# A state-space scan beside the products: places for ScalarE's part, for z's units and for small steps of the second block

## The reference

```python
xn = rmsnorm_2(x, norm1_w[l])
p = xn @ w_in[l]
z, xbc, dt_raw, p_rwkv, p_hgrn, p_gate = jnp.split(p, in_splits, axis=-1)
...
def ssd_chunked(x, dt, a, bm, cm):          # c = 4 chunks of Q = 128 tokens, both directions
    a_cum = jnp.cumsum(dt * a.reshape(G, hg), axis=2)
    xdt = x * dt[..., None]
    seg = a_cum[:, :, :, None] - a_cum[:, :, None]
    lmat = jnp.exp(jnp.where(mask, seg, -jnp.inf))
    cb = jnp.einsum('bcqgn,bcsgn->bcqsg', cm, bm)
    y_diag = jnp.einsum('bcqsgh,bcsghp->bcqghp', cb[..., None] * lmat, xdt)
    chunk_states = jnp.einsum('bcsgn,bcsghp->bcghpn', bm, xdt * decay_to_end[..., None])
    ...
y = y_f + y_b + xs * d_skip[:, None]
y = y.reshape(b, L, SSM_INNER) * jax.nn.silu(z)
...
p = p + mu[0] * (prev - p) + mu[1] * (nxt - p)      # token shift of p_rwkv
```

## Time and profile before

| | |
|---|---|
| median of 3 runs | 3432.21 us (3430.88 to 3433.6) |
| profiled execution | 3431.43 us, its span 3429.9 us |
| TensorE busy | 3310.9 us, 97% of the span |
| VectorE busy | 2018.7 us, 59% |
| ScalarE busy | 1354.2 us, 39% |
| granted clock of TensorE, mean | 0.992 |

### The profile page before, as it was taken

One profiled execution on the slowest core, in us unless ns is written; L12 is line 12 of the kernel. 1 busy time (PEld: TensorE's weight loads), 2 busy tenths in 40 slices (PEclk: granted clock), 3 DMA queues, 4 the chain that ended last, 5 costly groups with the idle time before them and its releaser, 6 DMA issues.

```text
span 3429.9 us, 53077 instructions
## 1 busy us (share of the span) xinstructions
PE 3310.9 (97%) x21864; PEld 2720.9 (79%) x21864; DVE 2018.7 (59%) x3803; ACT 1354.2 (39%) x2604; POOL 0.2 (0%) x4
## 2 busy tenths in 40 slices
PE   7989999999999999999999999999999999999998
PEld 7777788888888777788888888777777788888887
DVE  6776753554436776753554438775766678664434
ACT  5456543342225466543343224434443324232222
POOL 0000000000000000000000000000000000000000
PEclk9999999999999999999999999999999999999999
DMA  4221223233324221223233334333411235433332
GB/s 141 80 70 50 56 74 105 92 99 98 98 99 127 86 64 50 57 79 105 86 105 99 96 101 118 89 92 106 125 38 40 92 95 157 135 97 94 97 98 86
DMA packets 353875, 315.31 MB, mean 92 GB/s; under 512 B 10288, under 2 KB 281776, under 8 KB 353636
## 3 DMA queue, kind: packets, MB, share of 16 engines
q1 hardware_dynamic: 352916, 309.75, 29.9%
q10 hardware_dynamic: 720, 2.16, 0.2%
HBM read 288.28 MB, written 23.59 MB: 91 GB/s over the span
## 4 chain that ended last, share of the span: by engine, by line
PE 80%; DVE 11%; ACT 5%; issue 3%; DMA 2%; SPq 0%; DVEq 0%; ACTq 0%
PE banks L532 14%; PE banks L534 13%; PE banks L533 13%; PE banks L427 8%; PE banks L429 8%; PE banks L428 8%; DVE weights_r L368 2%; PE banks L632 1%; ACT weights_high_r L361 1%; PE banks L2928 1%; PE banks L2867 1%; PE banks L1241 1%; PE banks L1228 1%; PE banks L1332 1%; PE banks L2881 1%
## 5 line engine op out<-in xcount | busy, mean ns | idle before, releaser
L368 DVE TENSOR_TENSOR weights_r<-weights,weights_high_r 128x1024 fp32r<-128x1024 f32 (+2 forms) x517 | 592.9, 1154 | 355.7 <-ACT weights_high_r L361 354.6
L532 PE MATMUL banks<-h_T_hi,weights_high_r 128*128 128x512 f32 (+2 forms) x1912 | 759.6, 397 | 10.6 <-DVE h_T_lo L881 4.7
L534 PE MATMUL banks<-h_T_hi,weights_r 128*128 128x512 f32 (+2 forms) x1912 | 737.9, 386 | 0.0
L533 PE MATMUL banks<-h_T_lo,weights_high_r 128*128 128x512 f32 (+2 forms) x1912 | 737.5, 386 | 0.0
L361 ACT ACTIVATE weights_high_r<-weights 128x1024 fp32r<-128x1024 f32 (+2 forms) x517 | 511.2, 1000 | 360.8 <-DMA weights<-in_w_mlp 213.3
L532 PEld LDWEIGHTS banks<-h_T_hi,weights_high_r 128*128 128x128 f32 x1912 | 361.4, 189 | 98.6 <-issue 28.8
L534 PEld LDWEIGHTS banks<-h_T_hi,weights_r 128*128 128x128 f32 x1912 | 361.2, 189 | 72.7
L533 PEld LDWEIGHTS banks<-h_T_lo,weights_high_r 128*128 128x128 f32 x1912 | 361.7, 189 | 68.0 <-issue 2.6
L427 PE MATMUL banks<-weights_high_r,h_T_hi 128*128 128x512 f32 (+2 forms) x672 | 279.3, 416 | 9.2 <-DVE gate L2208 3.7
L429 PE MATMUL banks<-weights_high_r,h_T_lo 128*128 128x512 f32 (+2 forms) x672 | 254.9, 379 | 0.0
L428 PE MATMUL banks<-weights_r,h_T_hi 128*128 128x512 f32 (+2 forms) x672 | 254.7, 379 | 0.0
(11 more groups left out here) (562 smaller groups left out, 5228.5 us busy)
## 6 DMA issues: line engine op xcount, KB each, us to landing
weights<-in_w_in SPq DMA_DIRECT2D x183, 512.0 KB, 3.8
weights<-in_w_mlp SPq DMA_DIRECT2D x128, 512.0 KB, 3.8
weights<-in_ffn_w_in SPq DMA_DIRECT2D x44, 512.0 KB, 3.8
weights<-in_w_out SPq DMA_DIRECT2D x24, 512.0 KB, 3.6
weights<-in_ffn_w_down SPq DMA_DIRECT2D x22, 512.0 KB, 3.5
weights<-in_w_mem_kv SPq DMA_DIRECT2D x16, 512.0 KB, 3.5
weights<-in_w_diff_o SPq DMA_DIRECT2D x16, 512.0 KB, 3.6
weights<-in_w_mla_o SPq DMA_DIRECT2D x8, 512.0 KB, 3.4
```

What stands on the lines that cost most here:

```text
L368: ve.e.tensor_tensor(self.part(c.w_raw_r, u), self.part(c.w_raw, u), self.part(c.w_high_r, u).bitcast(F32), ALU.subtract).then_inc(*ve.tel ...
L532: pe.e.matmul(out, lhsT=wh[:, k, :], rhs=hi[k][:, cols], start=(k == 0), stop=False)
L533: pe.e.matmul(out, lhsT=wh[:, k, :], rhs=lo[k][:, cols], start=False, stop=False)
L534: mm = pe.e.matmul(out, lhsT=wl[:, k, :], rhs=hi[k][:, cols], start=False, stop=(k == self.chunks - 1))
```

## The change

It changes where steps stand in the order, and no arithmetic:

- `Tokens` gets `in_a_row`: for z, two units of weights are used for one tile before the next tile's turn (u0t0, u1t0, u0t1, u1t1 in place of u0t0, u0t1, u1t0, u1t1).
- ScalarE's part of the scan becomes a stage of its own, `StateDecays`, whose steps are at the time of TensorE's step plus 0.6. They stood at the time of VectorE's step, which is 3 or 2 steps ahead of TensorE's.
- The scan's times are written out: the first 0.53 steps earlier, and 4.02 apart in place of 4.07.
- The memsets of the shift's pads become a stage (`ShiftPads`) that stands 0.45 steps behind the convolution's end and ahead of the scan's L2552.
- The second step of `Constants2` stands at 7.2 in place of 3.1, and the last turn of the norm at 5.2 in place of 7.

```diff
-            for u in self.units:
+            for some_units in (self.units[j:j + self.in_a_row] for j in range(0, len(self.units), self.in_a_row)):
                 for t in some:
-                    yield n, u, t, t == some[0], u == self.units[-1]
+                    for u in some_units:
+                        yield n, u, t, t == some[0], u == self.units[-1]
...
-    def act(self):
+    def decays_act(self):
         ac = self.c.ac
         ac.wait_ge("dta_low")
...
+class StateDecays(Stage):
+    def __init__(self, ssm):
+        self.n, self.act = ssm.n, ssm.decays_act
...
+class ShiftPads(Stage):
+    n = 1
...
+    def dve(self):
+        self.shift.pads_dve()
+        yield
...
+    def pads_dve(self):
+        ve = self.c.ve
+        ve.wait_all(self.free)
+        for n, y in enumerate(self.pad):
+            ve.e.memset(y[:, 0:1], 0.0).then_inc(*ve.step())
+            ve.e.memset(y[:, S + 1:S + 2], 0.0).then_inc(*ve.tell("shift_padded", n))
...
-        plan.at(k, (0.6, 3.1, 18.2))
+        plan.at(k, (0.6, 7.2, 18.2))
...
+        plan.at(ShiftPads(shift), (plan.now + 0.45,))
...
-            return Tokens(c, name, c.hT, KD, w[:, col:col + 512], sink, ready=normed, ring=ring, together=2)
+            return Tokens(c, name, c.hT, KD, w[:, col:col + 512], sink, ready=normed, ring=ring, together=2, in_a_row=2 if how == "silu" else 1)
...
-        plan.beside(ssm, scan_at, plan.now - 1.5, [3] * 6 + [2] * (ssm.n - 6))
+        scan_times = [scan_at - 0.03 + 4.02 * n for n in range(ssm.n)]
+        scan_lags = [3] * 6 + [2] * (ssm.n - 6)
+        plan.at(ssm, scan_times, scan_lags)
+        plan.at(StateDecays(ssm), (t + lag + 0.6 for t, lag in zip(scan_times, scan_lags)))
...
-        self.block2 = Block2(c, plan, start, x_marks, hT_free, tile_times(-16, 4, 7, True), out[0])
+        self.block2 = Block2(c, plan, start, x_marks, hT_free, tile_times(-16, 4, 5.2, True), out[0])
```

More of the change, by code:

```diff
@@ L386, with __init__ @@
 class Tokens(Stage):
-    def __init__(self, c, tag, xT, chunks, src, sink, ready=(), tiles=NT, ring="gemm", together=NT, tile_ready=lambda t: ()):
+    def __init__(self, c, tag, xT, chunks, src, sink, ready=(), tiles=NT, ring="gemm", together=NT, tile_ready=lambda t: (), in_a_row=1):
         self.c, self.tag, self.xT, self.chunks, self.sink, self.ready, self.tiles = c, tag, xT, chunks, sink, ready, tiles
+        self.in_a_row = in_a_row
         self.ring, self.cols, self.tile_ready = ring, src.shape[1], tile_ready
@@ L2776, in __init__ @@
         self.pe, self.act, self.dve = ssm.steps_pe, ssm.steps_act, ssm.steps_dve
+class StateDecays(Stage):
[3 more added lines that the diff above has]
+    n = 1
+    def __init__(self, shift):
+        self.shift = shift
+    def dve(self):
+        self.shift.pads_dve()
+        yield
 class ShiftOut(Sink):
@@ L2798, in dve @@
         ve, x, dst, mu = self.c.ve, self.pad[f % 2], self.staging.cell("shift", f), self.k.v["rwkv_mu_2"]
[L2799 to L2803, removed]
         ve.wait_ge("emptied", *key)
```

## The result

The changed kernel took 3452.6 us in the median of four runs (3450.96 to 3453.0), the kernel before 3432.9 in four runs beside it (3430.88 to 3440.48). The ratio is 1.0046, 95% interval 1.0032 to 1.0059. The profiled executions are 3452.94 and 3431.43 us, with spans of 3451.5 and 3429.9: 21.6 us apart. The forecast was 3438.5 with a range of 3420 to 3447; the measured time lies 5.6 us above that range.

What follows compares the result with a forecast made beforehand. TensorE, 80% of what ended last, was taken to bound the kernel, so only its waits and clock count: waits +6.9, restarts -0.75, clock +0.9, together +7.0 on 3431.43, giving 3438.5 us, range 3420 to 3447.

Steps and rivals of the forecast that it cites:

- Head, pads: Last norm turn and shift pads' memsets: TensorE's waits of 1.97 (-2.0) and 1.92 (-1.9, its clock fall -1.7) go.
- D0: First scan group with inside terms (group D, chunk 0), near 2187 us: TensorE's wait grows from 1.40 to 5.4.
- E0 and F0: Groups E and F of scan chunk 0: their waits of 0.49 and 1.08 go, -1.6.
- The ring: Scan chunks 1 to 3: feature copy, decays, L361, L368 make seven group waits of 2.3 or 2.9, 17.3 us.
- E2: Group E of scan chunk 2: a TensorE wait of 2.3 us.
- E3: Group E of scan chunk 3: a TensorE wait of 2.3 us.
- G1: Group G of scan chunk 1: a wait of 0.4 us.
- z and gates: z products: the 3.39 wait goes, 1.53 becomes 1.2; the gates' first step meets an H group's adds, new wait 2.0.
- The sum of waits: TensorE's waits in the changed stretch: 26.3 us in 11 waits after, 19.4 in 16 before, so +6.9.
- The clock: TensorE's clock falls in the stretch: 7.7 x 1.7 = 13.1, less about 2 absorbed, less 10.3 now: +0.9.
- D: Rival: every wait brings a clock fall, or VectorE's decay products lengthen the cycle to 11.5: 3446 to 3450, chance 0.10.
- Rival C: VectorE's L368 does not bind in chunks 1 and 3, the 17.3 us of waits falls away: 3413 to 3424, chance 0.17.

Runs made afterwards that it cites:

- second trace: The changed kernel and the kernel before, each run once more unchanged to get another trace: 3457.32 us and 3439.91 us.

## Why the prediction was wrong

- **Head, pads: right for TensorE, one sign wrong.** There is no wait for L883 in the last turn and none for L2824's bank. But the first L2824 is still let go by a memset, 5.0 us earlier than before, where I had written that no memset would be its releaser:

```profile
2167.25 0.60 ACT L2824 ACTIVATE probabilities<-banks 128x512 f32<-128x512 f32 x1 [2.82 <-DVE probabilities L2815]
```

- **D0: right.** 5.45 for 5.4.
- **E0 and F0: right**, no wait in the trace of after.
- **The ring: right in place and size.** D1, E1, E2, D3 and E3 wait 2.23, 2.23, 2.21, 2.23, 2.23 for 2.3, F1 and F3 2.81 and 2.79 for 2.9. G1 0.34 for 0.4.
- **z and gates: right.** 1.54 for 1.2, and the gates' first step 2.23 for 2.0. As the forecast said, the 3.39 went with the decays' place.
- **The sum of waits: right to 1 us,** +8.0 for +6.9; what I had left out is 1.0 for L3350, ahead of the sums' matmuls, which the kernel before has too in its second trace.
- **The clock: this step failed.** "7.7 x 1.7 = 13.1, less about 2 ... less the 10.3 of now: +0.9". The number of falls was right (eight and nine for 7.7). The price of one was not: I took 1.7 from the falls of this stretch, though the stretch from 1199 to 1209 of the kernel before already showed one of 3.4:

```profile
1199.00:1209.00 10.00, 8.94 (x30) 6.70 (x31) 6.38 (x16) 5.07 (x13) 0.00 (x0) 0.66 0.18 53
```

  In the two traces of the changed kernel eight falls lost 20.5 us and nine lost 30.7, 2.6 and 3.4 each. Nor was 2 us of them absorbed beside the ring: the fall sits at the end of the wait and in the group and the step behind it that fills the bank, which is the ring's own path. From D1 at 2247.11 to E1 at 2260.90 it is 13.8 us, 10.7 and 3.1 of the fall's 3.4. What costs nothing is the part of a fall that lies inside the wait, 0.8 us in the first trace and 2.3 in the second. So the term is +10.3 (9.5 without that part) in place of +0.9, and +15.3 between the two second traces. The bound that I gave for it, +5, was too low even at one price: by its own words, 11 falls of 1.7 and nothing absorbed, it is 18.7 - 10.3 = +8.4, which would give 3446.
- **The restart of 0.15** for each wait has no row of its own. Behind a wait the eight matmuls of L2601 took 1.10 us for 1.00; the term is 0.75 us in the sum.
- **The base: low by chance.** The profiled execution of before lost 25.9 us to the clock over the whole span; its second trace lost 32.5. I left the median's 0.8 us aside and added to one execution. Outside the stretch the changed kernel's execution happened to lose 4.7 us more; without them it would be at 3448.2, still above the range. Among the runs beside the experiments the same kernel's span goes from 3428.5 us at a clock of 0.993 to 3441.9 at 0.990. For the changed kernel the four runs have 0.987 to 0.989.

Of the rivals D was nearest in kind, that every wait brings a fall. It came out not by the count (eight and nine, one of them in the sums' small matmuls), but by the length of each, and its 3446 to 3450 is too low as well. Rival C was no property of this change; it is what the kernel with the decays behind L361 does (3419.5, inside the 3413 to 3424 that C gave). The Trainium skill, "TensorE: Matmul & The Clock Gate", section "A second HAM failure mode: psum-queue depth-cycling", tells of a bf16 kernel in which frequent short idles between groups of matmuls make the clock go to and fro. I had given it too little weight: the traces here agree with it, for from 2180 to 2260 the granted clock is 0.91 and 0.88 in the two traces with the waits idle and 1.00 with them filled.

What stays open is whether a wait brings a fall and how long that is. The length of the wait doesn't decide it alone: E1's 2.2 us was followed by no fall in one execution and by one of 3.4 in another of the same kernel, F3's 2.8 by 3.4 and by none. Nor does every fall stand behind a wait: the kernel before has one at 2746 with no wait over 0.6 us in the 140 us ahead of it.

## What to carry to other kernels

When steps of several stages are laid out by times, check on each in-order engine what an instruction that waits for TensorE's next step now holds back. Here a feature's copy held the decays, they held the next weights' rounding, and VectorE's queue closed the ring, at 2.3 us for each group; moving the decays one place past the rounding took the kernel from 0.46% slower to 0.42% faster. In this kernel, which TensorE bounds, the waits of 2 us or more cost their length (24.4 us in nine) and for the clock two thirds of it again in one trace and all of it again in the other. So take the clock's price from several executions, and count the part of a fall behind the wait as lying on the path.

## What the runs showed of the hardware

- A fall of the clock loses 1.7 us or a multiple of it: 1.7, 3.4, 5.1 and once 6.8 us. Its length differs between executions of one kernel at the same place (E2: 1.7 and 3.4).
- The clock can fall while TensorE still waits: at D0 of the second trace it is 0.50 from 2183 to 2186, with TensorE at 0.00 us of work. That part of the loss costs no time.
- Filling the idle time with unneeded matmuls keeps the clock at 1.00 over 180 us (2180 to 2360) that had four and five falls in the two traces of the changed kernel; 0.5 to 0.7 us of idle at each of six groups brought none.
- Most of the spread of one kernel's runs goes with the clock: of 40 executions of the kernel before, those at 0.993 have spans of 3428.5 to 3429.7 us, those at 0.990 of 3434.8 to 3441.9.
- An fp32 matmul of 128x256 stands in the trace as two and takes about 0.45 us (nine in 4.05 us), twice what I had counted on.
